# Stages 2 and 3 of a two-block layer stack begin with token tile 0 alone, eight row tiles of h, then tile 1, then both

## The reference, cut to what matters

```python
    return rms_norm(x, final_norm_g)                     # first_block ends
...
        ada = jax.nn.silu(c) @ w_ada[l] + b_ada[l]       # second_block begins
        shift_m, scale_m, gate_m, shift_f, scale_f, gate_f = [
            t[:, None, :] for t in jnp.split(ada, N_MOD, axis=-1)]

        h = rms_norm_2(x, g_pre_mix[l]) * (1.0 + scale_m) + shift_m
        z = h @ w_in[l]
        c_q, c_kv, k_rope, q_g, k_g, v_g, a_g, r_g = split_cols(z, IN_SPLITS)
...
        x = x + gate_m * rms_norm_2(o, g_post_mix[l])

        h = rms_norm_2(x, g_pre_ffn[l]) * (1.0 + scale_f) + shift_f
        f = (jax.nn.silu(h @ w_ffn_gate[l]) * (h @ w_ffn_up[l])) @ w_ffn_down[l]
```

## Time and profile before

| | |
|---|---|
| median of 3 runs | 2262.06 us (2262.06 to 2263.79) |
| profiled execution | 2260.91 us, span 2258.6 us |
| TensorE busy | 2207.1 us (98%) |
| TensorE weight loads | 1886.4 us (84%) |
| VectorE busy | 1616.7 us (72%) |
| ScalarE busy | 1129.5 us (50%) |
| GpSimd busy | 24.1 us (1%) |

### The profile page before, as it was taken

How to read it: one execution, slowest core, us unless ns; L and a number is a source line. 1 busy time by engine, 2 the same in 40 slices (tenths; PEclk the granted TensorE clock), 3 DMA queues, 4 the chain that set the end, 5 groups by cost and what they waited for, 6 DMA issues and landing times.

```text
span 2258.6 us, 30610 instructions
## 1 busy us (share of the span) xinstructions
PE 2207.1 (98%) x12162; PEld 1886.4 (84%) x12162; DVE 1616.7 (72%) x2447; ACT 1129.5 (50%) x1691; POOL 24.1 (1%) x58
## 2 busy tenths in 40 slices
PE   7999999999999999999999998989999999999998
PEld 7999787788888888888879786877888888888987
DVE  6998885899998799998865666566555555554555
ACT  5434774555554455554454656544444444444443
POOL 1000000000000000000000000000000000000000
PEclk9999999999999999999999999999999999999999
DMA  8643436688889888889945551547776777655553
GB/s 278 206 167 129 149 94 214 201 291 288 292 296 359 322 275 290 284 281 341 336 161 190 178 176 57 180 142 233 227 232 220 233 226 231 220 190 187 186 186 122
DMA packets 137694, 500.97 MB, mean 222 GB/s; under 512 B 15472, under 2 KB 15616, under 8 KB 137040
## 3 DMA queue, kind: packets, MB, share of 16 engines
q1 hardware_dynamic: 136512, 494.43, 66.0%
q0 software_dynamic: 752, 2.49, 0.6%
q10 hardware_dynamic: 288, 2.10, 0.3%
HBM read 496.47 MB, written 2.49 MB: 221 GB/s over the span
## 4 chain that ended last, share of the span: by engine, by line
PE 91%; DVE 5%; ACT 2%; issue 1%; DMA 0%; POOL 0%; SPq 0%; DVEq 0%; POOLq 0%; ACTq 0%
PE bank L600 39%; PE both L600 27%; PE bank L592 20%; DVE w_lo L1614 2%; DVE conv_y L1720 1%; PE bank L817 1%; PE both L774 1%; PE bank L795 0%; DVE raw L1596 0%; PE bank L1100 0%; ACT w_hi L1142 0%; PE bank L645 0%; DVE x L2255 0%; DMA x<-x 0%; ACT junk L1155 0%
## 5 line engine op out<-in xcount | busy, mean ns | idle before, releaser
L1614 DVE TENSOR_TENSOR w_lo<-raw,w_hi 128x1024 fp32r<-128x1024 f32 x737 | 893.8, 1221 | 458.9 <-ACT w_hi L1142 457.3
L1142 ACT ACTIVATE w_hi<-raw 128x1024 fp32r<-128x1024 f32 x737 | 769.9, 1055 | 661.4 <-PE bank L600 389.9
L592 PE MATMUL bank<-h_both,w_hi 128*128 128x512 f32 x1408 | 494.7, 401 | 1.1 <-DVE h_both L1668 1.0
L592 PE MATMUL bank<-h_both,w_lo 128*128 128x256 f32 x1408 | 382.1, 282 | 0.0
L592 PEld LDWEIGHTS bank<-h_both,w_hi 128*128 128x128 f32 x1408 | 259.7, 189 | 58.9 <-DVE h_both L1668 1.4
L600 PE MATMUL bank<-w_hi,h_both 128*128 128x512 f32 (+2 forms) x1024 | 298.1, 372 | 2.2 <-DVE w_lo L1614 2.2
L600 PE MATMUL both<-w_hi,h_both 128*128 128x512 f32 (+1 forms) x960 | 294.6, 382 | 4.0 <-DVE h_both L1688 2.1
L592 PEld LDWEIGHTS bank<-h_both,w_lo 128*128 128x128 f32 x1408 | 266.8, 189 | 8.6
L600 PE MATMUL bank<-h_both,w_hi 128*128 128x256 f32 (+1 forms) x1312 | 243.5, 288 | 1.6 <-DVE w_lo L1614 1.0
L1596 DVE SCALAR_TENSOR_TENSOR raw<-raw,silu_c 128x1024 f32<-128x1024 f32 x192 | 233.9, 1218 | 7.6 <-ACT silu_c L1202 7.6
L600 PEld LDWEIGHTS bank<-w_hi,h_both 128*128 128x128 f32 x1024 | 187.3, 188 | 36.0 <-DVE w_lo L1614 3.2
(11 more groups left out here) (355 smaller groups left out, 2575.1 us busy)
## 6 DMA issues: line engine op xcount, KB each, us to landing
raw<-weights SPq DMA_DIRECT2D x924, 512.0 KB, 4.5
raw<-weights SPq DMA_DIRECT2D x5, 504.0 KB, 3.5
x<-x SPq DMA_DIRECT2D x2, 1024.0 KB, 5.8
bias<-bias_rows POOLq DMA_DIRECT2D x8, 256.0 KB, 10.0
silu_c<-c ACTq DMA_DIRECT2D x2, 1024.0 KB, 4.7
out<-x SPq DMA_DIRECT2D x8, 256.0 KB, 2.1
phase<-params SPq DMA_DIRECT2D x1, 497.0 KB, 10.5
raw<-weights SPq DMA_DIRECT2D x1, 488.0 KB, 4.5
```

Of the source, the lines that this page charges most:

```text
L592: t = e.matmul(into, s, a, start=opening, stop=closing)
L1142: e.activation(w_hi[:, n % PART_SLOTS, 0:widths[i]], raw[:, i % RAW_SLOTS, 0:widths[i]], ACT.Copy).then_inc(hi_ready, 1)
L1614: e.tensor_tensor(w_lo[:, slot, 0:widths[i]], raw[:, i % RAW_SLOTS, 0:widths[i]], w_hi[:, slot, 0:widths[i]].bitcast(F32), ALU.subtract).t ...
```

## The change: the order of the openings of stages 2 and 3

The first eight row tiles of h (the "head") are made per token tile, in four steps (`HEAD_STEPS`): tile 0 quarter 0, tile 0 quarter 1, tile 1 quarter 0, tile 1 quarter 1. A step is four transposes into one bank, four shifts of 128 columns and one rounding on ScalarE, and on VectorE one rounding and two rests, each for two row tiles of 128 tokens. TensorE does the first eight pieces of c_q, and of gate group 0, for tile 0, then the same eight for tile 1, then the other eight for both. In stage 2 the transposes of the first step come before the last trio of the group down1 (`before_last`).

The sequences of VectorE and ScalarE around it are written anew: the small products of the modulation vectors (`fold`) and rests of the first weight chunks move ahead, `normed(3, wide, (1,))` and `sum_final(1)` now stand among the steps of the head. In the last eight row tiles weight chunk k/2 - 1 is handled at even k from 10 on, instead of chunk k/2 at k. The row of the final gain for quarter 3 is in bank 1 instead of 0.

```diff
-        ROW_BANKS = ((4, 5, 7, 0), (4, 5, 7, 6), (4, 5, 7, 6))
+        HEAD = KD // 2
+        HEAD_STEPS = ((0, 0), (0, 1), (1, 0), (1, 1))
+        ROW_BANKS = ((4, 5, 7, 1), (4, 5, 7, 6), (4, 5, 7, 6))
 ...
+        def nth_chunk(stage, n):
+            return stream.splits[stream.split_no[FIRST_CHUNKS[stage]] + n]
 ...
-                order = [(at, None) for at in range(together)] + [(at, o) for o in range(2) for at in range(together, len(pieces))]
+                order = [(at, o) for o in range(2) for at in range(headwise)] + [(at, None) for at in range(headwise, together)] + [(at, o) for o in range(2) for at in range(together, len(pieces))]
                 for at_piece, only in order:
                     i, off, kt = pieces[at_piece]
                     k = kt - k0
-                    need(k)
+                    if before_last is not None and only == 1 and at_piece == len(pieces) - 1:
+                        before_last()
+                    if headwise:
+                        need(k, only)
+                    else:
+                        need(k)
-                        for b in out_banks:
-                            fill(b)
+                        for o, b in enumerate(out_banks):
+                            if only is None or only == o:
+                                fill(b)
 ...
+            def headed_steps(stage):
+                block_at = stage - 2
+                for i, (tt, q) in enumerate(HEAD_STEPS):
+                    b = TURN_BANKS[stage][i]
+                    w.wait_ge(scaled, 8 * stage + i + 1)
+                    fill(b)
+                    for at in range(4):
+                        t = e.transpose(banks[b][:, at * P:(at + 1) * P], wide[:, tt, (4 * q + at) * P:(4 * q + at + 1) * P], identity)
+                    t.then_inc(turned, 1)
+                    free[b] = h_shifted, 24 * block_at + 4 * i + 4
+                    yield
+                for k in range(HEAD, KD):
+                    b = TURN_BANKS[stage][k % 4]
+                    for tt in range(TT):
+                        w.wait_ge(scaled, 8 * stage + 2 * (k // 4) + tt + 1)
+                        fill(b)
+                        t = e.transpose(banks[b][:, tt * P:(tt + 1) * P], wide[:, tt, k * P:(k + 1) * P], identity)
+                    t.then_inc(turned, 1)
+                    free[b] = h_shifted, 24 * block_at + 16 + k - HEAD + 1
+                    yield
+            def headed_need(stage):
+                turning = headed_steps(stage)
+                done = [0]
+                base = 32 + 24 * (stage - 2)
+
+                def turn_until(steps):
+                    while done[0] < min(steps, 4 + KD - HEAD):
+                        next(turning)
+                        done[0] += 1
+
+                def need(k, tt=None):
+                    if k >= HEAD:
+                        turn_until(4 + k - HEAD + 4)
+                        w.wait_ge(h_ready, base + 16 + k - HEAD + 1)
+                        return
+                    if tt == 0:
+                        turn_until((1, 2, 2, 2, 2, 2, 3, 3)[k])
+                    else:
+                        turn_until((3, 4, 4, 4, 5, 6, 7, 8)[k])
+                    step = HEAD_STEPS.index((1 if tt is None else tt, k // 4))
+                    w.wait_ge(h_ready, base + 4 * step + 2 * (k % 4 // 2) + 2)
+
+                return need, lambda: turn_until(1)
 ...
-                    down = group_steps(("down1", half, n), 512, pair, ff_hi, ff_lo, ff_need, tilewise=TILEWISE if half and n == 3 else 0)
+                    ends = half and n == 3
+                    down = group_steps(("down1", half, n), 512, pair, ff_hi, ff_lo, ff_need, tilewise=TILEWISE if ends else 0, before_last=turn_first if ends else None)
 ...
-            need = h_need(2, lambda k: (h_shifted, k + 1))
-            group("c_q", Q_RANK, (0, 1), h_hi, h_lo, need)
+            need = need_mix2
+            group("c_q", Q_RANK, (0, 1), h_hi, h_lo, need, headwise=HEAD)
 ...
-            need = h_need(3, lambda k: (h_shifted, 16 + k + 1))
+            need, _ = headed_need(3)
 ...
-                    gating = group_steps(("gate", g), n, (0, 1), h_hi, h_lo, need)
+                    gating = group_steps(("gate", g), n, (0, 1), h_hi, h_lo, need, headwise=0 if g else HEAD)
 ...
-            def shift_h(stage, scale_v, shift_v):
-                for k in range(KD):
-                    if k in WITH_H[stage]:
-                        round_until(FIRST_CHUNKS[stage] + WITH_H[stage][k])
-                    w.wait_ge(turned, 16 * stage + k + 1)
-                    if k >= 4:
-                        w.wait_ge(h_ready, 16 * stage + k - 3)
-                    count = 16 * (stage - 2) + k + 1
+            def shift_head(stage, i, scale_v, shift_v):
+                tt, q = HEAD_STEPS[i]
+                block_at = stage - 2
+                w.wait_ge(turned, 32 + 12 * block_at + i + 1)
+                for pair in range(2):
+                    n, k0 = 2 * i + pair, 4 * q + 2 * pair
+                    if n >= 4:
+                        w.wait_ge(h_ready, 32 + 24 * block_at + 2 * (n - 4) + 2)
+                    for k in (k0, k0 + 1):
+                        e.activation(work2[:, n % 4, (k - k0) * P:(k - k0 + 1) * P], banks[TURN_BANKS[stage][i]][:, (k % 4) * P:(k % 4 + 1) * P], ACT.Identity,
+                                     scale=ada(scale_v)[:, k:k + 1], bias=ada(shift_v)[:, k:k + 1]).then_inc(h_shifted, 1)
+                w.wait_ge(h_shifted, 24 * block_at + 4 * i + 4)
+                e.activation(h_hi[:, k0:k0 + 2, tt * P:(tt + 1) * P], work2[:, n % 4, :].rearrange("p (k t) -> p k t", k=2), ACT.Copy).then_inc(h_rounded, 1)
+
+            def shift_tail(stage, scale_v, shift_v):
+                block_at = stage - 2
+                for k in range(HEAD, KD):
+                    if k > HEAD and k % 2 == 0:
+                        round_until(nth_chunk(stage, k // 2 - 1))
+                    w.wait_ge(turned, 32 + 12 * block_at + 4 + k - HEAD + 1)
+                    w.wait_ge(h_ready, 32 + 24 * block_at + (2 * (k - 4) + 2 if k - 4 < HEAD else 16 + k - 4 - HEAD + 1))
+                    count = 24 * block_at + 16 + k - HEAD + 1
 ...
-                        round_until(final["down1", 1, 3] + AHEAD - 1)
+                        round_until(c_first + 1)
+                        w.wait_ge(folded, 1)
+                        w.wait_ge(ada_ready, 2)
+                        shift_head(2, 0, 1, 0)
                         square_final("x3", (1,))
                         square_final("g3", (1,))
 ...
-            w.wait_ge(folded, 1)
-            w.wait_ge(ada_ready, 2)
-            shift_h(2, 1, 0)
+            for i in range(1, 4):
+                round_until(c_first + (2, 3, 3)[i - 1])
+                shift_head(2, i, 1, 0)
+            shift_tail(2, 1, 0)
 ...
-            shift_h(3, 4, 3)
+            for i in range(4):
+                round_until(gate_first + (1, 2, 3, 3)[i])
+                shift_head(3, i, 4, 3)
+            shift_tail(3, 4, 3)
 ...
             def factor_ffn2(n, tt):
                 w.wait_ge(row_factors, 6 + 2 * tt + 2)
-                w.wait_ge(x_gated, 2 * n + tt + 1)
+                w.wait_ge(x_gated, 2 * tt + n + 1 if n < 2 else 2 * n + tt + 1)
 ...
-            def shift_h(stage, scale):
-                scale_quarter(scale, 0, (1,))
-                if stage == 2:
-                    scale_quarter(scale, 1)
-                for k in range(KD):
-                    if stage == 2 and k in (2, 6):
-                        scale_quarter(scale, 2 + k // 4)
-                    if stage == 3 and k in (1, 4, 8):
-                        scale_quarter(scale, 1 + k // 4)
-                    if k in WITH_H[stage]:
-                        rests_until(FIRST_CHUNKS[stage] + WITH_H[stage][k])
+            def rest_pair(stage, i, pair):
+                tt, q = HEAD_STEPS[i]
+                block_at = stage - 2
+                n, k0, toks = 2 * i + pair, 4 * q + 2 * pair, slice(tt * P, (tt + 1) * P)
+                tmp = work2[:, n % 4, :].rearrange("p (k t) -> p k t", k=2)
+                if pair:
+                    w.wait_ge(h_rounded, 32 + 8 * block_at + i + 1)
+                else:
+                    w.wait_ge(h_shifted, 24 * block_at + 4 * i + 2)
+                    t = chain(e.tensor_copy(h_hi[:, k0:k0 + 2, toks], tmp))
+                    w.wait_ge(dve_step, t)
+                e.tensor_tensor(h_lo[:, k0:k0 + 2, toks], tmp, h_hi[:, k0:k0 + 2, toks].bitcast(F32), ALU.subtract).then_inc(h_ready, 2)
+
+            def rest_head(stage, i):
+                rest_pair(stage, i, 0)
+                rest_pair(stage, i, 1)
+
+            def rest_tail(stage, scale):
+                block_at = stage - 2
+                for k in range(HEAD, KD):
+                    if k == HEAD + 2:
+                        scale_quarter(scale, 3)
+                    if k > HEAD and k % 2 == 0:
```

(55 more changed lines are left out.)

18 lines of the change are left out of this document (11 added, 7 removed).

## The result

| | before | changed |
|---|---|---|
| median (us) | 2262.43 (2262.06 to 2263.79, 4 runs) | 2274.70 (2273.17 to 2275.79, 4 runs) |
| ratio | 1 | 1.0055 (1.0043 to 1.0066) |
| span of the profiled execution | 2258.6 | 2270.9 |
| TensorE busy | 2207.1 | 2213.1 |
| last matmul of down1 to the first of c_kv ("S2") | 34.30 | 42.81 |

The changed kernel is slower by 12.3 us; 2268.8 was forecast, in a range of 2261 to 2274. The direction was right, the size was 5.5 us short, and the median lies 0.7 above the range. S2 grew by 8.5 us and S3 by 2.8; four transposes that now stand ahead of the last trio of down1 add some 0.5, as foreseen. S2 and S3 are differences of starts in the timeline of TensorE (1146.46 to 1180.76 and 1501.46 to 1539.85 before; for the changed kernel the ends are in the next fence). They serve as the measure in all that follows, and each is read from one profiled execution.

What follows compares the result with a forecast made beforehand. TensorE carries 91% of the chain that ended last, so only time it loses counts. +6.0 us in stage 2 and +0.75 in stage 3 make +6.8; 2260.91 + 6.8 + 1.15 = 2268.8 us, range 2261 to 2274.

Steps and rivals of the forecast that it cites:

- The start of c_q: Stage 2's opening: TensorE starts c_q near 1148.9 after 1.7 us idle.
- The stall at k = 4: Stage 2, token tile 0: 5.3 us idle until 1157.4, released by `w_lo`, as the g3 square holds ScalarE.
- rival 3: Shifts and waits: narrow shifts at 0.25 and overlapping waits, each step 0.6 earlier; 2264.3 us, no change; chance 0.13.
- The stalls at k = 8 and k = 14: Stage 2's tail: 1.9 us idle at k = 8, 2.5 at k = 14, behind late weight chunks.
- Stage 3's k = 8: Start of stage 3's tail: 3.75 us idle behind a w_ada sum.
- The clock: Stage 2: one fall near 1156.7 after the 5.3 us gap, back near 1163.5; 2.8 us.
- Rival 2: Stage 3's tail: one more clock fall, behind the 3.75 us gap; 2271.8 us; chance 0.24.
- Stage 3 without it: Gate group 0: ends 0.75 us later, at 1540.6, with half clock at the head; without the half clock 0.
- The sum: Whole kernel: +6.0 us in stage 2 and +0.75 in stage 3 give +6.8, so 2268.8 us.
- Rival 1: Stage 2: the 5.3 us gap does not bring the clock down; 2266 to 2267 us; chance 0.15.
- Rival 4: Both stages: head works as the change says, half clock gone; -6.1 us, 2256.0; chance 0.12.
- The signs of being wrong: Stage 2: forecast wrong if k = 4 starts before 1155, or if the clock never falls there.

Runs made afterwards that it cites:

- the gaps filled: Changed kernel with unused matmuls of ones put into TensorE's gaps in stages 2 and 3, order unaltered: 2265.53 us.
- Both repairs: Changed kernel with old tail chunk order, step 1 of stage 2's head before the g3 square, and chunk c_first + 2's rest before sum_final(1): 2255.57 us.
- stage 2 alone: Kernel with the change in stage 2 (c_q) only, stage 3 in its old order: 2272.14 us.
- ScalarE's head order: Changed kernel with chunk c_first + 2's rounding and step 1 of stage 2's head moved ahead of token tile 1's g3 square on ScalarE: 2268.23 us.
- changed, two gaps filled: Changed kernel with matmuls of ones only ahead of k = 0 and k = 4 in stage 2, and k = 8 in stage 3: 2269.90 us.
- stage 3 alone: Kernel with the change in stage 3 (gate group 0) only, stage 2 in its old order: 2265.66 us.
- both orders and filled gaps: Changed kernel with the old tail chunk order, the repaired stage 2 head order, and matmuls of ones in the remaining gaps: 2253.74 us.
- the kernel before with filled gaps: Kernel before, nothing moved, with matmuls of ones in TensorE's waits at the openings of stages 1, 2 and 3: 2258.49 us.
- the kernel with the fault: Changed kernel with matmuls of ones in its gaps, where `idle(0)` by mistake also put a wait for bank 2 into every later use of h: 2281.33 us.

## Why the prediction was right in direction and wrong in size

- **The start of c_q.** Forecast 1148.9 after 1.7 us idle; 1149.44 in a trace whose down1 ended some 0.5 us later, 1.68 idle (1149.44 - 1147.76). Right.
- **The stall at k = 4.** Forecast 5.3 us, behind `w_lo`, by way of the g3 square; measured 4.85 between the last slot and the start (4.69 by the row), and the order on ScalarE, altered alone, took half of it away. Right, mechanism and size. Four narrow shifts take 1.48 us where I took 1.6, against 1.0 by rival 3: it falls. Its own sum was wrong too: eight steps of 0.6 us, half of them on the path, are 2.4 us and not the 4.5 that it takes off.
- **The stalls at k = 8 and k = 14.** Forecast 1.9 and 2.5; measured 2.02 and 2.43 between slot and start. Right, and undoing the chunk order removed both.
- **Stage 3's k = 8.** Forecast 3.75 behind a `w_ada` sum; 3.77. Right in size. With the chunk order undone the sum still stands ahead of the chunk and a gap of 0.78 is left, for a scaled tile; so the sum alone does not make the gap.
- **The clock, the step that failed.** My sum held "2.8 for the clock": one fall in stage 2, after the 5.3 us gap, of which it took 2.1 as the net loss. That fall came where I put it (1156.0 against near 1156.7) and cost 1.7. I put nothing for a fall behind the gaps of 1.9 and 2.5 us and gave no reason; the yardstick was the shortest wait with a fall behind it in the trace of before, 3.05 us, taken for a bound. Each of the two brought a stretch of 3.4 us, 1.6 us each. In all the clock cost stage 2 4.9 us (42.81 against 37.94 with the gaps filled) where the sum had 2.1. Without it the sum was right: +3.9 forecast, 37.94 + 0.5 - 34.30 = +4.1 measured.
- **Rival 2** was not a rival but came on top: the second fall in stage 3, behind the 3.77 us gap, was real. I priced it at 3.3 less 0.35; its stretch lasted 3.4 us and not 6.7, and it cost 1.55.
- **Stage 3 without it.** The forecast had 0.75 for the half clock at the head and nothing for stalls. Measured are 39.60 - 38.79 = 0.8 for the clock at the head and 38.79 - 38.39 = 0.4 for stalls.
- **The sum.** 6.8, and 3.0 more in stage 2 (2.8 clock, 0.2 stalls), and 2.0 in stage 3 (1.55 the second fall, 0.4 stalls) make 11.8 of the 12.3; most of the rest is the difference of profiled executions (the changed one was 0.4 us late already ahead of stage 1, 396.94 against 396.53 at the last out_attn matmul).
- **The other rivals.** Rival 1 (the long gap brings no fall) gave 2266 to 2267; with every gap filled it is 2265.5, which says again that the stalls were sized right. Rival 4 put its 2256.0 on one condition, that the square doesn't hold ScalarE. That condition alone gave 2268.23, with a wait of 2.34 us left at k = 4. Both repairs took 2255.57, but by other terms (the tail's gaps, which rival 4 kept, are gone; a fall in stage 3, which it dropped, stays): that the two numbers agree is luck.
- **The signs of being wrong.** Neither of the two that I named came. None of them asked for a second fall, so they could not catch this step.

The Trainium skill ("TensorE: Matmul & The Clock Gate", "HAM oscillation") tells of short bursts with a wait before each, which fall each time. The changed kernel goes that way further than I gave it credit for: five stretches in stages 2 and 3 against two. It agrees in part only, for here not each wait has a fall behind it.

Open: what decides whether a gap of about 2 us brings the clock down. Behind 1.85 us it fell in the changed kernel in two traces of two and with stage 2 alone, but not with ScalarE's head order nor with the head's gap filled; behind 2.25 us it fell in all but the first of these two. The trace of before had already shown that the length of a wait does not settle it. It has a fall with no wait of TensorE ahead of it, behind 32 narrow matmuls, and a wait of 2.18 us with the clock at full speed on both sides (two rows of the timeline, then a window as above):

```profile
199.25 3.77 PE L737 MATMUL bank<-kcmp,queries 128*128 128x30 f32 x32
...
241.54 0.50 PE L600 MATMUL bank<-w_hi,h_both 128*128 128x512 f32 x1 [2.18 <-DVE w_lo L1614]
...
202.50:203.00 0.50, 0.50 (x5) 0.50 (x5) 0.50 (x2) 0.00 (x0) 0.00 (x0) 0.64 0.11 41
```

That stretch, 202.6 to 206.0, comes back in 12 of the 14 traces and is missing in two, "stage 2 alone" and "changed, two gaps filled", though the program is the same up to there. It stays where the gaps of stages 2 and 3 are filled. The wait of 2.18 us comes back in all 14, never with a fall behind it. So the same work can have a fall behind it in one execution and none in another. The Trainium skill ("TensorE: Matmul & The Clock Gate", "What's actually happening") says that the windows in which the chip looks at activity run on by themselves and do not start with the kernel; where a gap lies in one would then count as well as its length. No run here shows the windows, so that is argued, not shown. Stage 3's own head (waits of 2.05 and 2.06 us) was not worked on. Except for the changed kernel, each kernel has one trace.

## What to carry to other kernels

Follow the engine that is queued behind, not the one that is sped up: one square that waits for another engine, standing ahead of four shifts, and one weight chunk moved two tiles later cost more than the shorter opening could give. After walking the stalls, price each of them a second time for the clock, also those of about 2 us, at half of the work in the stretch that may follow at most (1.6 us measured for one of 3.4 here, but 0.2 for one of 6.8 where VectorE and ScalarE set the pace). Where a stall can't be removed, cheap matmuls in it tell what the clock takes, and can pay by themselves (3 us here, without a change of order).

## What the runs showed of the hardware that I had not expected

- Gaps of 1.85 us and of about 2.25 us, each behind some 11 us and more of work, were often enough for a stretch at 1.2 GHz of 3.4 us (three traces of five, and five of six); behind the waits of 4.18 and 4.69 us of stage 2 it lasted 6.8 in every trace. In stage 3 the head's waits (2.05 and 2.06 us) and the gap of 3.77 us had stretches of 6.8 and 3.4 behind them in the full change, and of 3.4 and 6.8 with stage 3 alone.
- Executions of one kernel spread in part with it: with ScalarE's head order alone, one execution took 2267.17 us at a mean clock of 0.995 and the next 2271.48 at 0.991. With both orders and filled gaps the spread is 0.7 us (2253.51 to 2254.18) at 0.998. Filled gaps alone don't make it so small: the kernel before with filled gaps spreads over 3.6 us (2256.47 to 2260.03) at 0.998 to 0.999, which the clock does not explain. In the two traces without the stretch near 203 us TensorE was some 2 us earlier by the opening of stage 1 (398.43 us against 400.49 in the changed kernel).
- Matmuls whose only purpose is to be there hold the clock up. One of 128x128 in float32 takes 0.116 x 2 us (the row, of the kernel with the fault, shows 40 for 20):

```profile
1151.93 4.63 PE L676 MATMUL bank<-lasting 128*128 128x128 f32 x40
```
